# Attention outputs evicted by VectorE, the sinks' exponentials moved ahead, and the order of rows turned round in a scan

## What the reference computes

```python
# first block, two mixers: "a" (sliding window with sinks), then "b" (causal over all 256)
for i in range(2):
    hn = rmsnorm(h, norm_g[i])
    q, k, v, z = split_proj(hn, w_in, n_kv)        # 16 heads of 64; 2 or 4 key heads
    q, k = apply_rope(q), apply_rope(k)
    o = attention(q, k, v)                         # "a" adds exp(sink) to the denominator
    h = h + (o * silu(z)) @ w_out[i]
h = rmsnorm(h, final_g)
# second block, two hybrid layers
for layer in range(2):
    q, k, v, z, xbc, dt = split(rmsnorm(h) @ w_in)  # 8 heads, 2 key heads
    attn = dilated_attention(q, k, v)
    x, B, C = split(silu(causal_conv(xbc)))
    y = ssd_chunked(x, softplus(dt), -exp(a_log), B, C) + d_skip * x   # 2 chunks of 128 rows
    h = h + concat(attn, group_rmsnorm(y * silu(z))) @ w_out           # 2 groups of 8 heads
    h = h + (silu(hn @ w_gate) * (hn @ w_up)) @ w_down                 # hn = rmsnorm(h)
out = rmsnorm(h)
```

## Time and profile before

| | us |
|---|---|
| median of 3 runs | 910.14 |
| lowest and highest | 908.90, 911.51 |
| profiled execution | 908.58 |
| its span | 906.8 |

### The profile page before, as it was taken

How to read it: one execution, slowest core, us unless ns; L and a number is a source line. 1 busy time by engine, 2 the same in 40 slices (tenths; PEclk the granted TensorE clock), 3 DMA queues, 4 the chain that set the end, 5 groups by cost and what they waited for, 6 DMA issues and landing times.

```text
span 906.8 us, 12334 instructions
## 1 busy us (share of the span) xinstructions
PE 883.6 (97%) x4572; PEld 725.8 (80%) x4572; DVE 556.4 (61%) x972; ACT 518.4 (57%) x855; POOL 131.3 (14%) x102
## 2 busy tenths in 40 slices
PE   8999999999999999999999999999999999999996
PEld 5778788788877888888888887888887888888884
DVE  6745776548766677765555446656677755555443
ACT  5577566764777874554444333768865644444331
POOL 0032124221043430000000000053430000000000
PEclk9999999999999999999999999999999999999999
DMA  9632455424444423765555555443334665555521
GB/s 298 215 126 91 141 185 185 140 86 151 140 163 140 139 94 108 243 207 186 186 186 185 186 186 187 164 140 102 131 125 132 216 223 185 184 187 183 190 93 47
DMA packets 94736, 146.36 MB, mean 161 GB/s; under 512 B 6493, under 2 KB 54869, under 8 KB 94678
## 3 DMA queue, kind: packets, MB, share of 16 engines
q1 hardware_dynamic: 91424, 139.14, 46.5%
q0 software_dynamic: 1296, 4.72, 1.6%
q10 hardware_dynamic: 1958, 1.72, 0.5%
HBM read 144.52 MB, written 1.05 MB: 161 GB/s over the span
## 4 chain that ended last, share of the span: by engine, by line
PE 67%; issue 21%; DVE 6%; ACT 3%; DMA 1%; ACTq 1%; POOL 0%; SPq 0%; POOLq 0%; DVEq 0%
PE bank L1028 52%; PE bank L982 6%; PE bank L1169 1%; DVE lo L909 1%; PE bank L1080 1%; PE bank L1083 1%; PE bank L1105 1%; PE bank L1104 1%; DMA raw<-in_w_in_a 1%; PE bank L1103 1%; ACT hi L1196 1%; ACT junk L1222 1%; DVE hyb_MT L1801 1%; ACTq L1210 1%; PE bank L1148 0%
## 5 line engine op out<-in xcount | busy, mean ns | idle before, releaser
L909 DVE TENSOR_TENSOR lo<-raw,hi 128x1024 fp32r<-128x1024 f32 (+1 forms) x244 | 301.1, 1260 | 131.4 <-ACT hi L1196 129.3
L1196 ACT ACTIVATE hi<-raw 128x1024 fp32r<-128x1024 f32 (+1 forms) x260 | 266.5, 1056 | 83.2 <-PE bank L1028 72.8
L1028 PE MATMUL bank<-hi,xT_hi 128*128 128x512 f32 (+2 forms) x736 | 291.9, 397 | 3.0 <-DVE xT_lo L1632 1.0
L1028 PE MATMUL bank<-hi,xT_lo 128*128 128x512 f32 (+2 forms) x736 | 283.0, 385 | 0.0
L1028 PE MATMUL bank<-lo,xT_hi 128*128 128x512 f32 (+2 forms) x736 | 282.3, 384 | 0.0
L1028 PEld LDWEIGHTS bank<-hi,xT_hi 128*128 128x128 f32 x736 | 138.5, 188 | 36.2 <-issue 9.0
L1028 PEld LDWEIGHTS bank<-hi,xT_lo 128*128 128x128 f32 x736 | 138.4, 188 | 28.3
L1028 PEld LDWEIGHTS bank<-lo,xT_hi 128*128 128x128 f32 x736 | 138.7, 189 | 24.9 <-issue 0.5
L1028 PE MATMUL bank<-hi,hT 128*128 128x512 f32 x352 | 111.1, 395 | 0.0
L1028 PEld LDWEIGHTS bank<-hi,hT 128*128 128x128 f32 x352 | 66.3, 188 | 15.3
L1028 PE MATMUL bank<-lo,hT 128*128 128x512 f32 x176 | 69.4, 395 | 0.0
(11 more groups left out here) (237 smaller groups left out, 1024.3 us busy)
## 6 DMA issues: line engine op xcount, KB each, us to landing
raw<-in_w_in SPq DMA_DIRECT2D x26, 1024.0 KB, 5.0
raw<-in_w_gate SPq DMA_DIRECT2D x44, 512.0 KB, 3.7
raw<-in_w_up SPq DMA_DIRECT2D x44, 512.0 KB, 4.7
raw<-in_w_down SPq DMA_DIRECT2D x22, 1024.0 KB, 4.9
raw<-in_w_out SPq DMA_DIRECT2D x20, 1024.0 KB, 5.1
raw<-in_w_in_b SPq DMA_DIRECT2D x10, 1024.0 KB, 5.1
raw<-in_w_in_a SPq DMA_DIRECT2D x8, 1024.0 KB, 7.3
raw<-in_w_in_a SPq DMA_DIRECT2D x4, 256.0 KB, 5.1
```

Source lines behind the costliest of these rows:

```text
L909: return engine.tensor_tensor(lo[r][:, cols], raw[c.i % RAW][:, cols], hi[r][:, cols].bitcast(F32), ALU.subtract)
L1028: last = nc.tensor.matmul(bank[:, 0:wd], still[a], mv[r][:, off:off + wd], start=c.first and i == 0 and j == 0, stop=c.last and i == len(t ...
L1196: nc.scalar.activation(hi[c.i % SPLIT][:, cols], raw[c.i % RAW][:, cols], ACT.Copy)\
```

## The change

Four edits, made together.

1. `oev` is done by VectorE (a new step kind `vector_oev`, a plain copy) in all calls of mixers a and b, and in calls 3 and 5 of the hybrid layers.
2. The `sink` steps move from `fill_gates` into `attention`: the first half's behind call 4, the second half's behind call 8.
3. The angles, the sine, the tables and the exponential of a_log move to later steps: the four angle parts and the sine by one chunk (the sine to rest 13), the tables to chunk 21, a_log to scores 18.
4. In the hybrid layers' second scan group, the rows m = 1 are done before m = 0: `decay(1, 1, .)` and `scanned(1, 1)` change places with `decay(1, 0, .)` and `scanned(1, 0)`.

```diff
-ANGLES_AT = (("rest", 9), ("chunk", 10), ("rest", 10), ("chunk", 11))
-SINE_AT, TABLES_AT, ALOG_AT = 12, 14, 8
+ANGLES_AT = (("rest", 10), ("chunk", 11), ("rest", 11), ("chunk", 12))
+SINE_AT, TABLES_AT, ALOG_AT = 13, 21, 18
@@ attention
-        o = sc.step("oev", att=a, pair=head // 2, bank=a["obank"], pv=s)
-        a["obank"].freed = (o, "scalar")
+        by_vector = a["kind"] != "h" or n in (3, 5)
+        o = sc.step("vector_oev" if by_vector else "oev", att=a, pair=head // 2, bank=a["obank"], pv=s)
+        a["obank"].freed = (o, PARTS[o.kind][0])
@@ attention, at its end
+    if a["kind"] == "a" and n in (pairs // 2, pairs):
+        a["sinks"].append(sc.step("sink", att=a, half=len(a["sinks"])))
@@ fill_gates
-    es = sc.step("sink", att=a, half=half) if a["kind"] == "a" else None
+    es = a["sinks"][half] if a["kind"] == "a" else None
@@ hybrid
-        0: (do(decay, 1, 0, 0) + do(state, 1), do(decay, 1, 0, 1)),
-        1: (do(scanned, 1, 0) + do(turn_y, 0, 0), do(turn_y, 0, 1) + do(decay, 1, 1, 0) + do(decay, 1, 1, 1)),
-        2: (do(scanned, 1, 1) + do(group_norm, 1) + do(next_gain), ()),
+        0: (do(decay, 1, 1, 0) + do(state, 1), do(decay, 1, 1, 1)),
+        1: (do(scanned, 1, 1) + do(turn_y, 0, 0), do(turn_y, 0, 1) + do(decay, 1, 0, 0) + do(decay, 1, 0, 1)),
+        2: (do(scanned, 1, 0) + do(group_norm, 1) + do(next_gain), ()),
         3: (do(turn_y, 1, 0), do(turn_y, 1, 1))})
@@ VectorE's part
+            elif s.kind == "vector_oev":
+                B = Hb if s.att["kind"] == "h" else A
+                ended(dve, s.pv, "tensor")
+                W1 = HD + 1
+                src = psum[4 + s.bank.at][:, 0:4 * W1].rearrange("p (g m d) -> p m g d", g=2, m=2)
+                done(nc.vector.tensor_copy(B["o"][:, :, 2 * s.pair:2 * s.pair + 2, :], src), s)
```

More of the change, by code:

```diff
@@ L401, in new_attention @@
     a = sc.att = {"kind": which, "heads": heads, "nkv": nkv, "scores": [], "flip": [], "pv": [], "oev": [],
-                  "base": sc.heads, "tk": [], "tq": [], "gates": {}}
+                  "base": sc.heads, "tk": [], "tq": [], "gates": {}, "sinks": []}
     sc.heads += heads
@@ L684 @@
     "scores": ("tensor", "vector", "scalar"), "flip": ("tensor", "scalar", "vector"), "pv": ("tensor",),
-    "oev": ("scalar",), "sink": ("vector", "scalar"), "den": ("vector",), "gate": ("vector",), "pool_gate": ("gpsimd",), "pool_rope": ("gpsimd",),
+    "oev": ("scalar",), "vector_oev": ("vector",), "sink": ("vector", "scalar"), "den": ("vector",), "gate": ("vector",), "pool_gate": ("gpsimd",), "pool_rope": ("gpsimd",),
     "soft1": ("vector", "scalar"), "soft2": ("vector", "scalar"), "soft3": ("vector",),
@@ L1710, in _ @@
                 done(tt(esink[:, e, :], shift[:, e, :], spread(sinks[:, 0, e].unsqueeze(2), [P, 8, M]), ALU.add), s)
+            elif s.kind == "vector_oev":
[4 more added lines that the diff above has]
+                done(nc.vector.tensor_copy(B["o"][:, :, 2 * s.pair:2 * s.pair + 2, :], src), s)
             elif s.kind == "den":
                 B = Hb if s.att["kind"] == "h" else A
-                ended(dve, s.oev, "scalar")
+                ended(dve, s.oev, PARTS[s.oev.kind][0])
                 d = B["o"][:, :, 8 * s.half:8 * s.half + 8, HD]
```

## The result

The changed kernel takes 907.85 us (median of 13 runs, 906.32 to 908.45), the kernel before 909.91 in the same session (13 runs, 906.60 to 912.26). The ratio is 0.9978, with a 95% interval of 0.9968 to 0.9988: a small gain, but one that the interval tells from nothing. I had forecast 910.7, and had taken 2.7 us for the least that can be told from no change; the interval here is about 1 us to either side.

The account below looks back on a forecast made before the run. TensorE was taken to bound the kernel, busy 883.6 of 906.8 us, leaving only its pauses. Mixers +1.28 and +1.58, hybrids -2.79, sine +0.64, scan -0.10 gave +0.6 on 910.14: 910.7 us, 8-in-10 range 906.8 to 912.9.

Parts of the forecast that it names:

- the copy's 0.41: Output copy from PSUM on VectorE, 128x260: estimated at 0.41 us, with bounds 0.27 and 0.69.
- the lock-out by GpSimd: Calls 2 and 6 of the mixers: GpSimd's instruction keeps `lo` out altogether, so `lo` ends 1.08 us after it.
- calls 2, 5 and 6: Mixers' scores wait for the copy behind `lo`: 1.17, about 1.25, 1.04 us in a; 1.12, 0.93, 0.65 in b.
- the hybrids' -2.79: Call 3 of both hybrid layers: the pauses of 1.38 and 1.41 us go and nothing is given back.
- the gate's -0.90: Gate of mixer a's second half: TensorE's pause shrinks from 1.16 to 0.25 us, bounds 0 and -1.16.
- The first two rivals: Copies never held up by `lo`: 902.0, chance 0.05; only GpSimd collisions free, at calls 2 and 6: 906.7, chance 0.11.
- the lock-out of the copy by GpSimd: Rival: at call 6 of both mixers the copy waits for GpSimd's third instruction, +2.1 us, 912.8; chance 0.11.
- the scan's old wait: Pause of 0.95 us before the second scan group's transposes: forecast to go; rival that it stays: +1.9, 912.6, chance 0.04.
- the handover: From the end of VectorE's copy to TensorE seeing it: taken as 0.04 us.
- The sine's +0.64: Sine moved behind chunk 13 with its 1.28 us table load: new wait on xT_lo of 0.64 us, bounds 0 and 1.43.
- part 2: The prediction's part on sinks and angles: the gate's pause -0.90 us, the sine +0.64, tables and a_log 0.
- The scan's -0.05 a layer: Second scan group: the old pause of 0.95 us goes, a new wait on oT_lo of 0.90 comes; bounds -0.95 and +0.9.

Follow-up runs that it names:

- g1_narrow_pool: The changed kernel with GpSimd's rotation of the second queries and first-half gates cut to one head of eight, that output left out; 904.43 us.
- s1_angles: The kernel before with the angle work, sine, tables and a_log at their new places, sinks' exponentials where they were; 910.07 us.
- s2: The kernel before with only the sinks' exponentials of both halves moved, beside the last scores; 907.60 us.
- u2: The kernel before with only the second half's sinks' exponential moved beside its last scores; 907.60 us.
- u1: The kernel before with only the first half's sinks' exponential moved beside its last scores; 910.31 us.
- t1: The kernel before with the two loads of the convolution's taps and bias issued by GpSimd instead of ScalarE; 908.40 us.
- q1: The changed kernel with all the mixers' copies left on ScalarE; 903.09 us.
- t2: The changed kernel with the mixers' copies on VectorE at call 4 alone and the taps and bias loads issued by GpSimd; 901.21 us.
- p4_scan: The kernel before with the second scan group's later rows first, no other edit; 909.21 us.
- p3_sinks: The kernel before with the sinks' exponentials and the angle work at their new places, copies and scan order as before; 906.73 us.

## Why the prediction was wrong

**Right.** In the stretch, the mechanism: the bound (TensorE's pauses alone), the copy's 0.41, its place behind `lo`, the lock-out by GpSimd (1.08 forecast, 1.08 and 1.07 measured), calls 2, 5 and 6, the hybrids' -2.79 (-2.77), the gate's -0.90 (-0.94). The first two rivals fall with the six waits: the median lies near the second one's 906.7, by chance, for g1_narrow_pool shows that GpSimd's collisions do cost 3.7 us (3.98 in my sum); the lock-out of the copy by GpSimd falls with the rows of call 6, where the copy is done at 80.81 and GpSimd's instruction from 79.34 at 81.36; the scan's old wait did go. The mixers cost more than summed, by 0.3 and 0.4. Much of that is the handover, 0.12 where I had 0.04: each pause was 0.05 to 0.2 longer, and calls 4 and 7 of mixer a pay 0.1 each.

**The sine's +0.64** failed, in part 2, at "together with its table load of 1.28". I moved an instruction with the load that the trace showed before it, and didn't ask which load comes last ahead of it in the new order. s1_angles has that load and the wait, the changed kernel neither.

**The scan's -0.05 a layer** was mis-sized, at "`off` (0.51) comes before it and delays TensorE alike". It delays TensorE by 0.94, as it does the join, so the new wait is 0.5 and not 0.9: -0.4 a layer.

These two (-0.64 and -0.7) and the mixers (+0.7) bring the stretch from +0.6 to 0.0; that they partly cancel is luck. **The larger error is the step from the profiled execution to the median**: "on it the same +0.6 gives 910.7". It takes the time outside the stretch to be the same in both kernels. It is 46.8 before and 44.7 after, -2.05 us, and with the session's median of before (909.91 for 910.14) the account closes: 910.7 - 0.2 - 0.6 - 2.05 = 907.85 (it must, since the 2.05 is a difference of medians less stretches; what tests it are the runs). Shown is that moving the second half's sinks' step does it (s2, u2 against s1, u1), that two table loads go with that step, and that taking the loads of taps off ScalarE's queue gives 1.3 us by itself (t1). Not shown is why two table loads fewer (at 97.12 and 115.42 in before), some 70 us later in ScalarE's queue, shorten what two DMA issues take at 24 us. No run here could tell the number of loads from their places, and I leave it open.

**The better kernel** is the change without the mixers' copies but for call 4: 900.99 us, 7 us under the changed kernel. All copies on VectorE with `lo` behind them does nearly the same, 901.47.

## What to carry to other kernels

When an eviction moves to another engine, look first at what stands before it in that engine's queue. Here the copy was cheap and the place behind `lo` cost 6.4 us, which one change of order took away. When an activation moves, rebuild the list of table loads in the new order; a load doesn't belong to the instruction that it stood before. And when a gain of 0.2% is at stake, compare the stretches that the edits touch and the rest apart, over several programs: a span's difference of 0.7 us was nothing but the start.

## What the runs showed of the hardware

- From the first scores to the end two profiled executions of the kernel before took the same time to 0.06 us of 863 (863.16 and 863.10; 863.12 in t1_taps_gpsimd, edited ahead of it), and the parts added up to 0.1 us (858.43 for 858.4).
- Leaving out the end, where TensorE has run out of work, seventeen profiled executions hold six falls of its granted clock to 0.50 (1.2 GHz), each 3.4 us long: four between 8 and 12 us (before, q1, s2 and t2), two behind a pause of TensorE (617.00 in p4_scan, 67 to 69 in u1_sink_first). The last two made the stretch 1.5 and 1.6 us longer. The kernel before paused at the same place (0.34 and 0.29 us busy in the two microseconds from 617) and its clock stayed at 1.00.
- A DMA issue of 48 KB (the taps) on ScalarE's queue took 1.34 (p3_sinks) to 4.72 us (before) in the profiles; the same issue on GpSimd's took 0.55 (t1_taps_gpsimd).
- The start has two lengths, 2.1 us apart: the first large matmul begins at 10.8 us where four small matmuls at 4.27 took 2.1 to 2.3 us, and at 12.9 where they took 3.78.
- A `lo` (VectorE, two inputs in SBUF) and a GpSimd instruction kept each other out for whole instructions (`lo` 2.19 for 1.23, GpSimd 2.02 for 1.05 at call 6); a VectorE copy from PSUM ran at its 0.42 us beside that GpSimd instruction.
